# Expert walks: rounding the gated activations on ScalarE, with VectorE's remainder behind the first dot product

## The chip, the cores and the metric

The kernel runs on one core of a Trainium2 chip. The metric is device time in microseconds (us) of one execution. TensorE (PE) does the matrix products, VectorE (DVE) and ScalarE (ACT) the elementwise work, GpSimd (POOL) issues the indirect transfers and SyncE (SP) the plain ones. Each engine runs its own instructions in order and waits on semaphores for the others.

## What is computed

The reference is a two-layer backbone: in each layer a mixer (retention, convolution, long convolution) and then an expert layer over 16,384 single-neuron experts. The change touches the expert layer alone:

```python
q = (ht @ w_q).reshape(T, PEER_HEADS, 2, PEER_DKEY // 2)
...                                   # 16 experts for each of 8 heads: eb, with gates gb
def expert_block(args):
    hb, eb, gb = args
    a = jnp.einsum('tkd,td->tk', u_tab[eb], hb)
    w = (jax.nn.gelu(a.astype(jnp.float32)) * gb).astype(hb.dtype)
    return jnp.einsum('tk,tkd->td', w, v_tab[eb])
```

There are 512 latent tokens (and 256 context tokens in layer 0), each with 1024 features, all in 32-bit floats.

## The kernel before

The expert layer of each of the two layers is one stage, `stage_experts(l)`, which walks over NK = 128 blocks of 128 experts. 384 of the tokens are treated densely. For block k, `hidden(k)` multiplies the block of the u table with the activations (24 products of 128x384), ScalarE takes the gelu of the result into `w`, VectorE multiplies `w` by the dense gates `gt`, and `outputs(k)` multiplies it with the block of the v table and adds it up in six PSUM banks (18 products of 128x512). For accuracy every operand is split into two parts, a rounded one and its remainder: x_hi = round(x), x_lo = x - x_hi, and three products (hi hi, hi lo, lo hi) take the place of one. So a block needs `u_hi`/`u_lo`, `v_hi`/`v_lo` and `w_hi`/`w_lo`.

The remaining tokens are treated sparsely, in groups of 128: for each token the row of one chosen expert is gathered from memory (8 KB: its u and v parts), VectorE forms the dot product with the activation row (`dots`), ScalarE takes a small gelu and VectorE adds the weighted v part to the output row (`add_rows`). Layer 0 has two such groups (G = 2), layer 1 has one (G = 1). Four row buffers are in use, so a gather for step k+2 can be issued when `add_rows(k)` has read its buffer.

The order of the work is written out by hand for each engine, with waits on counted semaphores; there is no planner. In the steady part of the walk one step k is:

- VectorE, `step` (L2132): `weigh(k)` (gate product L2100, a drain, the rounding L2104 into `w_hi`, a drain, the remainder L2106 into `w_lo`, which raises `w_ready`), `dots(k)` (L2117, once for each group), `rest_u(k+2)` (L2085), `rest_v(k+1)` (L2090), `add_rows(k)` (L2125 and L2129, once for each group, which frees the row buffer).
- ScalarE, `step` (L2063): gelu of block k (L2067, waits for `hidden(k)`), `round_u(k+2)` (L2057, waits for the load of the u block), small gelu (L2071, waits for `dots(k)`), `round_v(k+1)` (L2061, waits for the load of the v block).
- TensorE, `step`: `hidden(k+1)`, then `outputs(k)`, which waits for `v_split` and `w_ready`.
- SyncE, `step` (L1984): load of the u block k+2 (L1987, 512 KB) once `hidden(k)` is done; load of the v block k+1 (L1991, 512 KB) once `outputs(k-1)` is done; and in every second step (k odd) a load of the gates for two blocks (L1981, 384 KB) once `w_ready` shows that `weigh(k)` is done. SyncE waits in this order, so the u load of the next step stands behind the wait of the gate load.
- GpSimd: G gathers (L2014), 1 MB each, each waiting for its row buffer.

Below, a *gate step* is a step k in which a gate load is issued (k odd), and a *plain step* is one in which none is. The u and v blocks have two buffers each.

The wait that ties the u load to the gate load is in these lines:

```python
if k % 2 == 1 and at_most(b, k, NK - 4):
    sp.wait_ge(w_ready.sem, w_ready.at(b + (k + 1)))
    load_gates(b, k + 3)
```

Of the kernel before, what the change touches and what calls it, by code (L numbers as in the profile page):

```python
# [7 lines left out]
F32 = mybir.dt.float32  # L8
U32 = mybir.dt.uint32
F32R = mybir.dt.float32r  # L10
ALU = mybir.AluOpType
# [45 lines left out]
def build(nc, xT, cT, ctxT, final_g, ada, mix, peer_u, peer_uv, peer_rows, peer_v, par, hw1, hw2, hw3, keys, k_mats, k_rope,  # L57
          k_dec, k_decc, k_feat_x, k_feat_c, k_win_x, k_win_c, k_dft_x, k_dft_c, out):
    stack = ExitStack()
    with stack:  # L60
# [13 lines left out]
        def new(name):  # L74
            return Count(nc, stack, name)
# [26 lines left out]
        rows_free, dots_ready, gelu_ready = new("expert_rows_free"), new("dots_ready"), new("small_gelu_ready")  # L102
        ctx_in, ctx_free, ctx_gelu = new("ctx_slots_loaded"), new("ctx_rows_free"), new("ctx_gelu_ready")
        ctx_rows_in = [new(f"ctx_rows_loaded_{k}") for k in range(6)]
        a_ready, a_free, o_done = new("hidden_ready"), new("hidden_read"), new("outputs_done")

        def flat(at, n):
# [1840 lines left out]
        def stage_experts(l):  # L1948
# [20 lines left out]
            def at_most(b, k, n):  # L1969

                return not isinstance(b, int) or b + k < n
# [5 lines left out]
            with nc.Block() as block:  # L1977
# [75 lines left out]
                @block.scalar  # L2053
                def _(act):
                    def round_u(b, k):
                        act.wait_ge(loaded[k % 2].sem, loaded[k % 2].at(8 * b + (16 * (k // 2) + 16)))
                        act.activation(u_ring_hi[:, k % 2, :], ring[:, k % 2, :], ACT.Copy).then_inc(u_hi.sem, 1)  # L2057

                    def round_v(b, k):
                        act.wait_ge(loaded[2 + k % 2].sem, loaded[2 + k % 2].at(8 * b + (16 * (k // 2) + 16)))  # L2060
                        act.activation(v_ring_hi[:, k % 2, :], ring[:, 2 + k % 2, :], ACT.Copy).then_inc(v_hi.sem, 1)  # L2061

                    def step(b, k):  # L2063
                        act.wait_ge(a_ready.sem, a_ready.at(b + (k + 1)))
                        if past(b, k, 2):
                            act.wait_ge(w_ready.sem, w_ready.at(b + (k - 1)))
                        act.activation(w[:, k % 2, :], ps[:, 6 + k % 2, 0:TD], ACT.Gelu_apprx_tanh).then_inc(a_free.sem, 1)  # L2067
                        if at_most(b, k, NK - 2):
                            round_u(b, k + 2)
                        act.wait_ge(dots_ready.sem, dots_ready.at(b + (k + 1)))  # L2070
                        act.activation(slot_g[:, G * k:G * k + G], slot_a[:, G * k:G * k + G], ACT.Gelu_apprx_tanh)\  # L2071
                           .then_inc(gelu_ready.sem, 1)
                        if at_most(b, k, NK - 1):
                            round_v(b, k + 1)

                    round_u(0, 0)
                    round_u(0, 1)
                    round_v(0, 0)
                    walk(act, step)

                @block.vector
                def _(dve):
                    def rest_u(b, k):
                        dve.wait_ge(u_hi.sem, u_hi.at(b + (k + 1)))
                        dve.tensor_tensor(ring_lo[:, k % 2, :], ring[:, k % 2, :], u_ring_hi[:, k % 2, :].bitcast(F32), ALU.subtract)\  # L2085
                           .then_inc(u_split.sem, 1)

                    def rest_v(b, k):
                        dve.wait_ge(v_hi.sem, v_hi.at(b + (k + 1)))
                        dve.tensor_tensor(ring_lo[:, 2 + k % 2, :], ring[:, 2 + k % 2, :], v_ring_hi[:, k % 2, :].bitcast(F32),  # L2090
                                          ALU.subtract).then_inc(v_split.sem, 1)

                    def weigh(b, k):

                        if k % 2 == 0:
                            half = (k // 2) % 2
                            dve.wait_ge(gates_in[half].sem, gates_in[half].at(4 * b + 16))
                        dve.wait_ge(a_free.sem, a_free.at(b + (k + 1)))
                        x, hi = w[:, k % 2, :], w_hi[:, k % 2, :]
                        dve.tensor_tensor(x, x, gt[:, (k // 2) % 2, k % 2, :], ALU.mult)  # L2100
                        dve.drain()
                        if past(b, k, 2):
                            dve.wait_ge(o_done.sem, o_done.at(b + (k - 1)))
                        dve.tensor_copy(hi, x)  # L2104
                        dve.drain()
                        dve.tensor_tensor(w_lo[:, k % 2, :], x, hi.bitcast(F32), ALU.subtract).then_inc(w_ready.sem, 1)  # L2106

                    def row_of(k, g):
                        return (G * k + g) % NBUF

                    def dots(b, k):

                        for g in range(G):
                            sem = rows_in[row_of(k, g)]
                            turn = 16 * ((G * k + g) // NBUF) + 16
                            dve.wait_ge(sem.sem, sem.at((16 * G // NBUF) * b + turn))
                            last = dve.tensor_tensor_reduce(rows[row_of(k, g)][:, 0:D], rows[row_of(k, g)][:, 0:D], h_rows[g], 1.0, 0.0, ALU.mult, ALU.add,  # L2117
                                                            slot_a[:, G * k + g:G * k + g + 1])
                        last.then_inc(dots_ready.sem, 1)

                    def add_rows(b, k):

                        dve.wait_ge(gelu_ready.sem, gelu_ready.at(b + (k + 1)))
                        here = slice(G * k, G * k + G)
                        dve.tensor_tensor(slot_w[:, here], slot_g[:, here], gates[:, ds(b + k, 1), :].rearrange("p a g -> p (a g)"),  # L2125
                                          ALU.mult)
                        dve.drain()
                        for g in range(G):
                            dve.scalar_tensor_tensor(o_rows[g], rows[row_of(k, g)][:, D:2 * D], slot_w[:, G * k + g:G * k + g + 1],  # L2129
                                                     o_rows[g], ALU.mult, ALU.add).then_inc(rows_free.sem, 1)  # L2130

                    def step(b, k):  # L2132
                        weigh(b, k)
                        dots(b, k)
                        if at_most(b, k, NK - 2):
                            rest_u(b, k + 2)
                        if at_most(b, k, NK - 1):
                            rest_v(b, k + 1)
                        add_rows(b, k)

                    rest_u(0, 0)
                    rest_u(0, 1)
                    rest_v(0, 0)
                    walk(dve, step)
            for k in range(4):
                loaded[k].add(16 * NK // 2)
            place[0] += 4
            for c in (a_ready, a_free, o_done, u_hi, v_hi, u_split, v_split, w_ready, dots_ready, gelu_ready):
                c.add(NK)
            for g in gates_in:  # L2150
                g.add(16 * NK // 4)
# [201 lines left out]
```

## Time and profile before

| | us |
|---|---|
| median of 3 runs | 6430.33 |
| the three runs | 6427.9, 6433.2, 6430.33 |
| the profiled execution, time | 6423.93 |
| the profiled execution, span from first to last instruction | 6422.1 |

| engine | busy us | share of the span | instructions |
|---|---|---|---|
| PE, products | 5309.5 | 83% | 24102 |
| PE, weight loads | 4083.9 | 64% | 24102 |
| DVE | 4402.1 | 69% | 7633 |
| ACT | 1714.8 | 27% | 2929 |
| POOL | 1100.2 | 17% | 824 |

The page also cuts the span into 40 equal slices of about 160 us and gives a digit for the busy tenths of each engine. The walk of layer 0 lies in slices 16 to 23, where the memory traffic stands at 370 to 372 GB/s; the walk of layer 1 lies in the last eight slices, at about 270 GB/s. Everything else (mixers, choice of experts, filters) is left as it is by the change.

### The profile page before, as it was taken

How to read it: one execution, taken by the hardware profiler on the slowest of the kernel's cores; microseconds unless marked ns; L12 is line 12 of the kernel's file. 1: busy time of each engine (PE TensorE's matmuls, PEld its weight loads, DVE VectorE, ACT ScalarE, POOL GpSimd, SP SyncE). 2: the span in 40 equal slices, each digit the busy share in tenths (PEclk: the TensorE clock that was granted, in tenths of full speed). 3: DMA queues.
4: the chain of work that ended last, by engine and by line, in shares of the span. 5: the costliest groups of instructions: out<-in, count | busy, mean ns of one | idle time of the engine just before them, and what ended most of it. 6: DMA issues, size and time to landing. Idle time of an engine off the chain costs nothing. (4 is left out here: it accounts for less than half of the span.)

```text
span 6422.1 us, 71090 instructions
## 1 busy us (share of the span) xinstructions
PE 5309.5 (83%) x24102; PEld 4083.9 (64%) x24102; DVE 4402.1 (69%) x7633; ACT 1714.8 (27%) x2929; POOL 1100.2 (17%) x824
## 2 busy tenths in 40 slices
PE   7787827887887777999999878977886559999998
PEld 5385726633355566888888737723475448999897
DVE  1347576758785787999999832358344987777776
ACT  1132211121022354222222211221022553333333
POOL 0003005505342001333333200005000001111110
PEclk8897868988998878999999979978998669999999
DMA  6141317701574356999999712201121247777775
GB/s 207 70 151 54 113 44 292 263 29 46 181 257 145 105 152 227 372 372 372 372 370 371 307 69 76 91 14 52 52 79 59 53 105 266 273 272 273 271 274 199
DMA packets 465497, 1180.24 MB, mean 184 GB/s; under 512 B 225436, under 2 KB 259645, under 8 KB 412543
## 3 DMA queue, kind: packets, MB, share of 16 engines
q1 hardware_dynamic: 373186, 641.52, 29.4%
q0 software_dynamic: 92160, 536.91, 22.3%
q8 instruction: 70, 1.15, 0.1%
q14 instruction: 81, 0.66, 0.0%
HBM read 1114.09 MB, written 64.23 MB: 183 GB/s over the span
## 5 line engine op out<-in xcount | busy, mean ns | idle before, releaser
L2014 POOL DMA_INDIRECT arena<-in_peer_uv,kept x384 | 522.2, 1360 | 3027.5 <-DVE arena L2129 1630.8
L220 PE MATMUL psum<-h_hi,ring_lo 128*128 128x384 f32 x2048 | 692.8, 338 | 0.0
L220 PE MATMUL psum<-h_lo,u_ring_hi 128*128 128x384 f32 x2048 | 692.3, 338 | 0.0
L220 PE MATMUL psum<-h_hi,u_ring_hi 128*128 128x384 f32 x2048 | 689.5, 337 | 0.0
L220 PE MATMUL psum<-v_ring_hi,w_hi 128*128 128x512 f32 x1536 | 618.5, 403 | 56.0 <-DVE w_lo L2106 56.0
L220 PE MATMUL psum<-ring_lo,w_hi 128*128 128x512 f32 x1536 | 605.2, 394 | 0.0
L220 PE MATMUL psum<-v_ring_hi,w_lo 128*128 128x512 f32 x1536 | 600.9, 391 | 0.0
L2057 ACT ACTIVATE u_ring_hi<-kept 128x1024 fp32r<-128x1024 f32 x256 | 271.7, 1062 | 1064.7 <-DMA kept<-in_peer_u 1052.7
L2129 DVE SCALAR_TENSOR_TENSOR arena<-arena 128x1024 f32<-128x1024 f32 x384 | 482.1, 1283 | 19.2
L2117 DVE CUSTOM_DVE_ANT_0 arena<-arena 128x1024 f32<-128x1024 f32 x384 | 458.8, 1220 | 0.1
L2090 DVE TENSOR_TENSOR ring_lo<-kept,v_ring_hi 128x1024 fp32r<-128x1024 f32 x256 | 313.7, 1226 | 202.6 <-ACT v_ring_hi L2061 191.9
L1629 PE MATMUL psum<-arena 128*128 128x128 f32 x1536 | 286.8, 346 | 147.8 <-DVE arena L1713 91.8
L220 PEld LDWEIGHTS psum<-h_hi,u_ring_hi 128*128 128x128 f32 x2048 | 384.6, 188 | 11.5 <-issue 0.5
L220 PEld LDWEIGHTS psum<-h_lo,u_ring_hi 128*128 128x128 f32 x2048 | 384.3, 188 | 10.8 <-issue 0.5
L220 PEld LDWEIGHTS psum<-v_ring_hi,w_hi 128*128 128x128 f32 x1536 | 289.0, 188 | 150.0 <-issue 94.4
L220 PEld LDWEIGHTS psum<-h_hi,ring_lo 128*128 128x128 f32 x2048 | 384.2, 188 | 0.0
L1110 PE MATMUL psum<-arena,kept 128*128 128x512 f32 (+1 forms) x768 | 305.8, 560 | 80.9 <-DVE arena L1156 63.9
L1629 PEld LDWEIGHTS psum<-arena 128*128 128x128 f32 x1536 | 248.8, 247 | 187.8 <-DVE arena L1713 128.7
L2085 DVE TENSOR_TENSOR ring_lo<-kept,u_ring_hi 128x1024 fp32r<-128x1024 f32 x256 | 312.9, 1223 | 47.9 <-ACT u_ring_hi L2057 47.1
L220 PEld LDWEIGHTS psum<-v_ring_hi,w_lo 128*128 128x128 f32 x1536 | 289.3, 188 | 70.2
L220 PEld LDWEIGHTS psum<-ring_lo,w_hi 128*128 128x128 f32 x1536 | 288.5, 188 | 53.5
L2061 ACT ACTIVATE v_ring_hi<-kept 128x1024 fp32r<-128x1024 f32 x256 | 269.7, 1053 | 180.4 <-DMA kept<-in_peer_uv 180.0
(343 smaller groups left out, 10444.2 us busy)
## 6 DMA issues: line engine op xcount, KB each, us to landing
kept<-in_mix SPq DMA_DIRECT2D x312, 512.0 KB
kept<-in_peer_u SPq DMA_DIRECT2D x256, 512.0 KB
kept<-in_peer_uv SPq DMA_DIRECT2D x256, 512.0 KB
kept<-in_ada SPq DMA_DIRECT2D x96, 512.0 KB
gate_scratch<-arena SPq DMA_DIRECT2D x12, 4096.0 KB, 20.8
arena<-gate_scratch SPq DMA_DIRECT2D x128, 384.0 KB
arena<-in_k_dft_x SPq DMA_DIRECT2D x6, 2048.0 KB
spec_scratch<-arena SPq DMA_DIRECT2D x4, 2048.0 KB, 8.5
```

Source lines behind the costliest of these rows:

```text
L220: done = pe.matmul(out, lhs[x], rhs[y], start=first and j == 0, stop=last and j == 2)
L1110: last = pe.matmul(ps[:, k, 0:T], ring[:, k, kc * P:(kc + 1) * P], x[:, kc, :], start=kc == 0, stop=kc == KC - 1)
L1629: last = pe.matmul(ps[:, n % 4, q * P:(q + 1) * P], hot_j[n % 3][:, q, :], hot_i[n % 3][:, q, :], start=True, stop=True)
L2014: pool.indirect_dma_start(rows[q % NBUF], None, peer_uv, bass.IndirectOffsetOnAxis(ap=row_id[q % G][:, q // G:q // G + 1], axis=0))\
L2057: act.activation(u_ring_hi[:, k % 2, :], ring[:, k % 2, :], ACT.Copy).then_inc(u_hi.sem, 1)
L2061: act.activation(v_ring_hi[:, k % 2, :], ring[:, 2 + k % 2, :], ACT.Copy).then_inc(v_hi.sem, 1)
L2085: dve.tensor_tensor(ring_lo[:, k % 2, :], ring[:, k % 2, :], u_ring_hi[:, k % 2, :].bitcast(F32), ALU.subtract)\
L2090: dve.tensor_tensor(ring_lo[:, 2 + k % 2, :], ring[:, 2 + k % 2, :], v_ring_hi[:, k % 2, :].bitcast(F32), ALU.subtract).then_inc(v_split.s ...
L2117: last = dve.tensor_tensor_reduce(rows[row_of(k, g)][:, 0:D], rows[row_of(k, g)][:, 0:D], h_rows[g], 1.0, 0.0, ALU.mult, ALU.add, slot_a[: ...
L2129: dve.scalar_tensor_tensor(o_rows[g], rows[row_of(k, g)][:, D:2 * D], slot_w[:, G * k + g:G * k + g + 1], o_rows[g], ALU.mult, ALU.add).th ...
```

## The change

ScalarE does the rounding into `w_hi` as a Copy activation of the same 128x384 tile, right after its gelu and ahead of `round_u(k+2)`; it waits for a new semaphore `weighed` that VectorE's gate product raises. VectorE's rounding and both drains of `weigh` are gone. The remainder `w_lo` becomes a function of its own, `rest_w`, which waits for a second new semaphore `w_rounded` and stands after the first dot product of the step: between the two dot products in layer 0 (G = 2), after the only one in layer 1 (G = 1). `w_ready` is raised by it as before. The wait for `outputs(k-2)`, which guards `w_hi`, moves with the rounding to ScalarE.

```diff
@@ ScalarE, step
                         act.activation(w[:, k % 2, :], ps[:, 6 + k % 2, 0:TD], ACT.Gelu_apprx_tanh).then_inc(a_free.sem, 1)
+                        act.wait_ge(weighed.sem, weighed.at(b + (k + 1)))
+                        if past(b, k, 2):
+                            act.wait_ge(o_done.sem, o_done.at(b + (k - 1)))
+                        act.activation(w_hi[:, k % 2, :], w[:, k % 2, :], ACT.Copy).then_inc(w_rounded.sem, 1)
                         if at_most(b, k, NK - 2):
                             round_u(b, k + 2)
@@ VectorE, weigh
                         dve.wait_ge(a_free.sem, a_free.at(b + (k + 1)))
-                        x, hi = w[:, k % 2, :], w_hi[:, k % 2, :]
-                        dve.tensor_tensor(x, x, gt[:, (k // 2) % 2, k % 2, :], ALU.mult)
-                        dve.drain()
-                        if past(b, k, 2):
-                            dve.wait_ge(o_done.sem, o_done.at(b + (k - 1)))
-                        dve.tensor_copy(hi, x)
-                        dve.drain()
-                        dve.tensor_tensor(w_lo[:, k % 2, :], x, hi.bitcast(F32), ALU.subtract).then_inc(w_ready.sem, 1)
+                        x = w[:, k % 2, :]
+                        dve.tensor_tensor(x, x, gt[:, (k // 2) % 2, k % 2, :], ALU.mult).then_inc(weighed.sem, 1)
+
+                    def rest_w(b, k):
+                        dve.wait_ge(w_rounded.sem, w_rounded.at(b + (k + 1)))
+                        dve.tensor_tensor(w_lo[:, k % 2, :], w[:, k % 2, :], w_hi[:, k % 2, :].bitcast(F32), ALU.subtract)\
+                           .then_inc(w_ready.sem, 1)
@@ VectorE, dots
                         for g in range(G):
+                            if g == 1:
+                                rest_w(b, k)
@@ VectorE, step
                         dots(b, k)
+                        if G == 1:
+                            rest_w(b, k)
```

## Rows read from the trace of the kernel before

**Rows 1.** Busy time by engine in a stretch of each walk: PE, PEld, DVE, ACT, POOL
```profile
2528.00:3653.00 1125.00, 1076.25 (x5249) 941.87 (x5248) 1083.94 (x1500) 323.33 (x499) 382.08 (x251) 1.00 0.96 371
5300.00:6300.00 1000.00, 993.97 (x4962) 897.46 (x4963) 744.61 (x1069) 316.15 (x474) 124.24 (x121) 1.00 0.78 272
```

**Rows 2.** Waits in 2700 to 3600 us: who for whom, total us, times, longest
```profile
PE psum L220 <- DVE w_lo L2106: 39.2, 100, 0.8
...
DVE ring_lo L2085 <- ACT u_ring_hi L2057: 0.6, 2, 0.5
```

**Rows 3.** Timeline of VectorE, gate step at 2689.76, plain step at 2698.75: start, duration
```profile
2689.76 0.55 DVE L2100 TENSOR_TENSOR arena<-arena 128x384 f32<-128x384 f32 x1
2690.38 0.45 DVE L2104 CAST w_hi<-arena 128x384 fp32r<-128x384 f32 x1
2690.91 0.56 DVE L2106 TENSOR_TENSOR w_lo<-arena,w_hi 128x384 fp32r<-128x384 f32 x1
2691.38 1.22 DVE L2117 CUSTOM_DVE_ANT_0 arena<-arena 128x1024 f32<-128x1024 f32 x1
...
2692.53 1.22 DVE L2117 CUSTOM_DVE_ANT_0 arena<-arena 128x1024 f32<-128x1024 f32 x1
...
2693.67 1.22 DVE L2085 TENSOR_TENSOR ring_lo<-kept,u_ring_hi 128x1024 fp32r<-128x1024 f32 x1
...
2698.75 0.55 DVE L2100 TENSOR_TENSOR arena<-arena 128x384 f32<-128x384 f32 x1
...
2702.66 1.22 DVE L2085 TENSOR_TENSOR ring_lo<-kept,u_ring_hi 128x1024 fp32r<-128x1024 f32 x1
...
2707.74 0.55 DVE L2100 TENSOR_TENSOR arena<-arena 128x384 f32<-128x384 f32 x1
```

**Rows 4.** Timeline of SyncE's queue in the same gate step
```profile
2691.64 0.38 SPq L1981 DMA_DIRECT2D arena<-gate_scratch  x1
2692.55 0.33 SPq L1987 DMA_DIRECT2D kept<-in_peer_u  x1
```

**Rows 5.** Timeline of ScalarE in the same two steps
```profile
2690.05 1.06 ACT L2057 ACTIVATE u_ring_hi<-kept 128x1024 fp32r<-128x1024 f32 x1 [3.72 <-DMA kept<-in_peer_u]
...
2701.30 1.06 ACT L2057 ACTIVATE u_ring_hi<-kept 128x1024 fp32r<-128x1024 f32 x1 [5.97 <-DMA kept<-in_peer_u]
```

**Rows 6.** Timeline: first and last of 61 gate steps, and the u load behind each
```profile
2545.77 0.55 DVE L2100 TENSOR_TENSOR arena<-arena 128x384 f32<-128x384 f32 x1
...
2557.65 1.06 ACT L2057 ACTIVATE u_ring_hi<-kept 128x1024 fp32r<-128x1024 f32 x1 [6.31 <-DMA kept<-in_peer_u]
...
3626.45 0.55 DVE L2100 TENSOR_TENSOR arena<-arena 128x384 f32<-128x384 f32 x1
...
3638.16 1.06 ACT L2057 ACTIVATE u_ring_hi<-kept 128x1024 fp32r<-128x1024 f32 x1 [6.16 <-DMA kept<-in_peer_u]
```

**Rows 7.** Line L1917: ScalarE's Copy of 128x384, ns min/median/max
```profile
L1917 ACT ACTIVATE h_hi<-arena x16: 506/509/526, 2480.5 to 5281.7; 128x384 fp32r<-128x384 f32 x16
```

**Rows 8.** Timeline of layer 1's SyncE queue: two u loads in a row
```profile
5806.53 0.33 SPq L1987 DMA_DIRECT2D kept<-in_peer_u  x1
...
5814.90 0.33 SPq L1987 DMA_DIRECT2D kept<-in_peer_u  x1
```

**Rows 9.** Memory traffic (last two columns) within the two steps of rows 3
```profile
2690.76:2692.76 2.00, 1.63 (x8) 1.17 (x7) 1.93 (x5) 0.36 (x1) 1.32 (x1) 1.00 0.80 215
2695.76:2707.76 12.00, 11.62 (x61) 10.52 (x60) 11.55 (x17) 2.59 (x4) 3.92 (x3) 1.00 1.01 405
```

**Rows 10.** GpSimd's second gather in the gate step of rows 3
```profile
2690.95 1.32 POOL L2014 DMA_INDIRECT arena<-in_peer_uv,kept  x1 [0.30 <-issue]
```

**Rows 11.** Gate step at 3013.93, its second gather, and the u load behind it
```profile
3013.93 0.55 DVE L2100 TENSOR_TENSOR arena<-arena 128x384 f32<-128x384 f32 x1
...
3015.81 1.78 POOL L2014 DMA_INDIRECT arena<-in_peer_uv,kept  x1 [0.98 <-issue]
...
3023.50 1.06 ACT L2057 ACTIVATE u_ring_hi<-kept 128x1024 fp32r<-128x1024 f32 x1 [4.00 <-DMA kept<-in_peer_u]
```

More of the change, by code:

```diff
@@ L104, in build @@
         ctx_rows_in = [new(f"ctx_rows_loaded_{k}") for k in range(6)]
+        weighed, w_rounded = new("hidden_weighed"), new("hidden_rounded")
         a_ready, a_free, o_done = new("hidden_ready"), new("hidden_read"), new("outputs_done")
@@ L2147, in stage_experts @@
             place[0] += 4
-            for c in (a_ready, a_free, o_done, u_hi, v_hi, u_split, v_split, w_ready, dots_ready, gelu_ready):
+            for c in (weighed, w_rounded, a_ready, a_free, o_done, u_hi, v_hi, u_split, v_split, w_ready, dots_ready, gelu_ready):
                 c.add(NK)
```

## The prediction

> **What bounds the kernel now.** The change lies in the two expert walks, so I read the busy time of each engine in a stretch of either walk first. In layer 1 TensorE is busy 994 of 1000 us and VectorE 745: TensorE is the bound [rows 1]. In layer 0 VectorE is busy 1084 of 1125 us, TensorE 1076, and the transfer engines stand at a share of 0.96: three resources within a few per cent of full [rows 1]. The waits show the order among them: TensorE waits for `w_lo` in every step (39.2 us in 100 steps, 0.39 each), VectorE for a rounded u block only twice [rows 2]. Before the change, layer 0 therefore runs at the speed of VectorE's own list.
>
> The timeline of VectorE gives that list: from the gate product of one step to that of the next it is 8.99 us, almost without a gap [rows 3]. Over 120 steps the mean is (3626.45 - 2545.77) / 120 = 9.005 [rows 6], so 18.01 us for a gate step and a plain step together. This pair is the unit below, since SyncE's list repeats every two steps.
>
> The last view is the one that decides: when does each u block land, against when it is wanted? The u block whose load is issued in the plain step is rounded from 2690.05 to 2691.11 and its remainder starts at 2693.67, 2.6 us to spare [rows 3, 5]. The u block whose load stands behind the gate load is another matter: issued at 2692.55 [rows 4], landed at 2701.30, rounded by 2702.36, wanted by VectorE at 2702.66 [rows 3, 5]: 0.30 us to spare. Measured from the gate product of its gate step it lands 11.54 us later; in the first and the last of 61 such pairs the distance is 11.88 and 11.71 [rows 6], and the mean over the 61 is 11.56.
>
> **The change, part by part.**
>
> *VectorE's list.* Before, gate product to `rest_u` is 3.91 us: 0.62 to the rounding, 0.53 to the remainder, 0.47 to the first dot product, 1.15 and 1.14 for the two [rows 3]. After, the gate product hands over after 0.47 (the start-to-start of the equal tensor-tensor L2106), then 1.15, the remainder 0.47, and 1.14: 3.23. So 0.68 us fewer, and the list needs 8.99 - 0.68 = 8.31. The two new waits hold it up only if ScalarE is late: the Copy of this shape takes 0.51 [rows 7]; from 0.55 it is done at about 1.15, the remainder is due at 1.62. ScalarE is busy 323 of 1125 us [rows 1] and waits at that moment for a u block or for `dots`; 0.51 more costs nothing.
>
> *TensorE.* Its floor is layer 1's period, 5814.90 - 5806.53 = 8.37 [rows 8]. `w_ready` comes 2.18 us after the gate product (0.47 + 1.15 + 0.56) instead of 1.71: 0.47 later. In the steady state that alone is harmless, since the gate product itself may come earlier.
>
> *SyncE, the queue that the change is moved past.* The gate load waits for `w_ready`, and the next u load stands behind it. Both are issued 0.47 later after the gate product: the gate load at 2.35 instead of 1.88 [rows 3, 4].
>
> *The u block behind the gate load, new bound.* After it lands, 1.06 us of rounding and about 0.04 of hand-over pass, and from that `rest_u` to the gate product of the next gate step it is 2707.74 - 2702.66 = 5.08 [rows 3]. With L as the distance from gate product to landing, a pair cannot be shorter than L + 1.10 + 5.08. With the old L of 11.56 that is 17.74 us. VectorE's 16.62 and TensorE's 16.74 are out of reach: most of the 1.36 us that VectorE saves in a pair becomes waiting for this block. The question is only whether L keeps still. Call its shift x; a pair is then 17.74 + x, against 18.01 before, and the point of no change is x = 0.27.
>
> *What moves L.* First, the later gate load. Around it the traffic is only 215 GB/s, while from 6 to 18 us of the pair it is 405 at a full share [rows 9]. 0.47 us at the lower rate instead of the full one delays (405 - 215) / 405 x 0.47 = 0.22 us of transfer; the ends are 0 (the gathers use the gap fully) and 0.47. Second, the plain step now begins 8.31 instead of 8.99 us after the gate product, and its two gathers of 1 MB each with it, 0.68 us earlier, while the u block is still in flight. If the gathers took the whole traffic in that time, the block would land 0.68 later; if its bytes were already through, 0. I take two thirds, 0.45: a gather's row is 8 KB against 4 KB for a row of the block. That this order matters, one row shows: in the gate step at 3013.93 the second gather started 1.88 instead of 1.19 us after the gate product, and the u block landed 9.57 instead of 11.56 us after it [rows 10, 11]. A gather 0.7 us later gave 2.0 us; the mirror image, the gathers relatively earlier by as much, is the far end of x, 0.22 + 2.0 = 2.2.
>
> So x = 0.22 + 0.45 = 0.67, a pair 18.41. There are 62 pairs with a gate load (k odd up to 123): 62 x 0.40 = +25 us.
>
> A page of the Trainium skill, "DMA: Bandwidth & Descriptors", section "Where 436 GB/s comes from", holds that transfers from HBM are bound at about 358 GB/s for a core, which speaks against any gain here; by that rule a step with its 3.34 MB would take 9.3 us, before and after. The trace does not agree: it holds 371 over 1125 us and 405 over 12 us [rows 1, 9]. The measurement decides, and the bound is taken from 405.
>
> *Ends of the walks.* In the last step of each walk TensorE has nothing left but `outputs`, and the 0.47 lies open: +1 us for both. *Layer 1.* TensorE is full there and its period stays; VectorE's idle 25% hides the later `w_ready`. 0.
>
> **Sum.** +25 + 1 = +26 us. The profiled execution took 6423.93 (span 6422.1), 6.4 below the median; its own time would become 6450, and the median 6430.33 + 26 = 6456.
>
> **The rivals.**
>
> 1. *The full gain.* The u block follows the faster step, as if its landing were tied to VectorE's list, and layer 0 becomes bound by TensorE like layer 1: 125 steps x (9.005 - 8.37) = 79 us, less 1: 6352. For it: traffic of 3.34 MB in 8.37 us is 399 GB/s, under 405. Against it: 0.30 us to spare [rows 3 to 5] where 0.68 a step would be needed twice, less what the load gives. Chance 0.08.
> 2. *The landing keeps still* (x near 0, under 0.06): a pair of 17.74, 62 x 0.27 = 17 us less, plus 1: 6414. For it: a landing set by bytes, not by the moment of issue. Chance 0.17.
> 3. *A balance* (x from 0.06 to 0.46): within 13 us of before. The removed VectorE time is found again as VectorE's wait for the u block. A traffic that is already full gives the same, 6431: the trace's 371 GB/s over the walk may be all that this mix of transfers reaches, against the 405 over 12 us [rows 1, 9]; I give that 0.05 of this rival's chance of 0.25. The bandwidth rule of the Trainium skill's "DMA: Bandwidth & Descriptors" would come out as this case.
> 4. *The forecast, the other side of 1 and 2:* one mechanism, the u load queued behind the gate load, with its price x above 0.46. Chance 0.50, of which 0.08 for more than +65 us (x over 1.3).
>
> That ScalarE's rounding be late enough to hold VectorE at `rest_w` is excluded by 0.5 us of room a step.
>
> **How the numbers follow.** The likeliest is the forecast, 6456; its own range is 6443 to 6495. With the balance and the small gain, and with the far end of x cut where 0.08 is left, the range is 6405 to 6495; the full gain is left out. About 0.2%, 13 us, is what a measurement of this kernel can tell from no change: faster 0.25, same 0.25, slower 0.50.
>
> **What the changed profile would show.** Right: VectorE's L2085 waits for L2057 in about every second step, about 1.8 us each, in all over 100 us in the layer-0 walk; the list from gate product to `rest_u` takes 3.23 in gate steps; gate and plain steps differ (8.3 and 10.1); TensorE waits for `w_lo` still; layer 1 keeps 8.37. Wrong: L2085 without waits and a period near 8.4 (rival 1); L at or under 11.56 (rival 2); waits at `rest_w` for the rounding; or waits for v blocks in layer 0, which showed none and which I have not priced.

## The result and the profile after

The change makes the kernel slower by over 3%, some eight times the loss that was forecast.

| | before | after |
|---|---|---|
| median, us | 6428.87 (6 runs, 6419.52 to 6433.2) | 6631.62 (6 runs, 6606.17 to 6644.68) |
| ratio, with its 95% interval | | 1.0318 (1.0302 to 1.0334) |
| span of the profiled execution, us | 6422.1 | 6624.1 |
| mean granted clock of TensorE | 0.895 | 0.889 |

Busy time by engine in a stretch of each walk, after (columns PE, PEld, DVE, ACT, POOL, granted clock, transfer share, GB/s), to be held against [rows 1]:

```profile
2528.00:3653.00 1125.00, 985.67 (x4620) 869.55 (x4619) 901.69 (x1211) 337.61 (x550) 333.27 (x221) 0.94 0.88 326
5500.00:6400.00 900.00, 852.64 (x4214) 759.34 (x4215) 584.53 (x807) 302.15 (x504) 101.07 (x100) 1.00 0.73 256
```

In layer 0 no resource is full any more: TensorE fell from 1076 to 986 us, VectorE from 1084 to 902, the traffic from 371 to 326 GB/s. Layer 1 had TensorE at 99%; it is at 95% now. When everything has room and the time is longer, the kernel runs at the speed of a loop of latencies. The granted clock, full before, is 0.94 in layer 0.

The step periods say how much is lost where. A *pair* is a gate step and the plain step behind it; all periods here are means over 62 gate and 62 plain steps, read from the gate products in the timeline.

| us | gate step | plain step | pair | against before, x 62 |
|---|---|---|---|---|
| layer 0 before | 8.99 | 9.02 | 18.01 | |
| layer 0 after | 8.31 | 12.00 | 20.31 | +142 |
| layer 1 before | 7.93 | 8.83 | 16.76 | |
| layer 1 after | 6.44 | 11.35 | 17.79 | +64 |

Together +206, where the spans differ by 202. The waits in the layer-0 walk (2700 to 3600 us; who for whom, total us, times, longest) name what is late, where before there were 0.39 us a step for `w_lo` and nearly nothing else [rows 2]:

```profile
PE psum L221 <- DVE w_lo L2109: 111.7, 43, 4.1
ACT v_ring_hi L2062 <- DMA kept<-in_peer_uv: 108.0, 37, 5.6
DVE ring_lo L2095 <- ACT v_ring_hi L2062: 105.3, 37, 5.5
DVE ring_lo L2090 <- ACT u_ring_hi L2058: 61.9, 44, 1.6
```

and in layer 1 (5400 to 6300 us):

```profile
DVE ring_lo L2095 <- ACT v_ring_hi L2062: 167.6, 46, 4.1
DVE ring_lo L2090 <- ACT u_ring_hi L2058: 124.2, 49, 3.6
...
PE psum L221 <- DVE w_lo L2109: 44.0, 44, 1.7
```

Once a pair, VectorE waits for the u block, then for the v block, and then TensorE for `w_lo`. The wait for the v block is the larger one in both walks.

One pair of layer 0 in the timeline (start, duration; SPq and POOL rows are issues of transfers), the gate step at 3141.66 and the plain step at 3149.95, against [rows 3 to 5]. At 22.53 us it is one of the longer pairs; the mean is 20.31. Where a load is said to land, it is the start of ScalarE's rounding, which waits for it; where ScalarE did not wait, that is only the latest time at which it can have landed.

```profile
3141.66 0.55 DVE L2105 TENSOR_TENSOR arena<-arena 128x384 f32<-128x384 f32 x1
...
3142.25 0.52 ACT L2072 ACTIVATE w_hi<-arena 128x384 fp32r<-128x384 f32 x1 [4.01 <-DVE arena L2105]
...
3143.28 0.55 DVE L2109 TENSOR_TENSOR w_lo<-arena,w_hi 128x384 fp32r<-128x384 f32 x1
...
3143.97 0.47 PE L221 MATMUL psum<-v_ring_hi,w_hi 128*128 128x512 f32 x1 [2.13 <-DVE w_lo L2109]
...
3145.48 0.63 PE L221 MATMUL psum<-ring_lo,w_hi 128*128 128x512 f32 x1
3145.90 0.63 PE L221 MATMUL psum<-v_ring_hi,w_lo 128*128 128x512 f32 x1
...
3149.33 0.39 PE L221 MATMUL psum<-ring_lo,w_hi 128*128 128x512 f32 x1
3149.56 0.39 PE L221 MATMUL psum<-v_ring_hi,w_lo 128*128 128x512 f32 x1
3149.79 0.34 PE L221 MATMUL psum<-h_hi,u_ring_hi 128*128 128x384 f32 x1
...
3150.14 0.33 SPq L1992 DMA_DIRECT2D kept<-in_peer_uv  x1
...
3159.33 1.06 ACT L2062 ACTIVATE v_ring_hi<-kept 128x1024 fp32r<-128x1024 f32 x1 [4.87 <-DMA kept<-in_peer_uv]
...
3160.42 1.23 DVE L2095 TENSOR_TENSOR ring_lo<-kept,v_ring_hi 128x1024 fp32r<-128x1024 f32 x1 [4.79 <-ACT v_ring_hi L2062]
...
3164.19 0.55 DVE L2105 TENSOR_TENSOR arena<-arena 128x384 f32<-128x384 f32 x1
```

Read it as a ring. `w_ready` comes 2.17 us after the gate product (3143.83). 0.14 later the outputs start and take 5.82. The v load goes out 0.35 after them, lands after 9.19, is rounded and waited for in 1.09, and 3.77 later stands the gate product of the next gate step. 2.17 + 0.14 + 5.82 + 0.35 + 9.19 + 1.09 + 3.77 = 22.53, the whole of 3164.19 - 3141.66. Such a sum of distances closes by itself. What makes the ring the bound is that each link starts only when the one before it ends: the rows show TensorE idle for `w_lo` (2.13 us), ScalarE for the v block (4.87) and VectorE for ScalarE (4.79), and VectorE runs from `rest_v` to the next gate product almost without a gap. It goes once round in two steps, because the v block that is loaded is the one for two blocks later.

The outputs need 5.82 us instead of 18 x 0.234 = 4.21 because the clock is low at their head: their products start 0.43 apart until 3147.6 and 0.23 apart after. By stretches of the same pair:

```profile
3141.66:3144.66 3.00, 0.87 (x5) 0.58 (x4) 3.00 (x6) 1.47 (x2) 2.20 (x2) 0.95 0.52 176
3144.66:3149.95 5.29, 5.29 (x18) 4.21 (x17) 5.14 (x7) 1.53 (x3) 0.84 (x1) 0.70 0.97 327
3149.95:3164.19 14.24, 12.59 (x66) 11.49 (x65) 8.23 (x12) 3.12 (x5) 3.04 (x3) 1.00 0.85 318
```

The granted 0.70 in the middle is a mixture of the two levels, 1.2 and 2.4 GHz, behind an idle TensorE. This is not so in every pair: in 27 of the 62 the outputs took 5.6 to 7.0 us, all behind a wait of TensorE of 2.1 us or more, and in the other 35 they took 4.24.

With the full clock the ring is 11.73 us + the time of the v landing in layer 0. In layer 1 the list behind the v block is shorter (2.57 for 3.77) and `w_ready` comes at 2.16, so it is 10.53 + landing. Here is where layer 1's time goes (a gate step at 6003.47):

```profile
6003.82 1.01 POOL L2015 DMA_INDIRECT arena<-in_peer_uv,kept  x1 [11.01 <-DVE arena L2135]
...
6009.62 1.01 POOL L2015 DMA_INDIRECT arena<-in_peer_uv,kept  x1 [4.79 <-DVE arena L2135]
...
6010.36 0.33 SPq L1992 DMA_DIRECT2D kept<-in_peer_uv  x1
...
6018.16 1.06 ACT L2062 ACTIVATE v_ring_hi<-kept 128x1024 fp32r<-128x1024 f32 x1 [3.96 <-DMA kept<-in_peer_uv]
```

and the same in the kernel before:

```profile
5810.89 1.01 POOL L2014 DMA_INDIRECT arena<-in_peer_uv,kept  x1 [7.96 <-DVE arena L2129]
...
5818.64 1.01 POOL L2014 DMA_INDIRECT arena<-in_peer_uv,kept  x1 [6.73 <-DVE arena L2129]
...
5819.06 0.33 SPq L1991 DMA_DIRECT2D kept<-in_peer_uv  x1
...
5823.70 1.06 ACT L2061 ACTIVATE v_ring_hi<-kept 128x1024 fp32r<-128x1024 f32 x1 [1.52 <-DMA kept<-in_peer_uv]
```

The gathers follow each other after 7.75 us before and after 5.80 us now, and the v block takes 7.80 instead of 4.64. Over the walk: of 60 v blocks that ScalarE waited for after the change all took more than 6 us, and 59 of them had a gather 0.7 us ahead of the load and, 5.8 us ahead of that, the gather before it. Before, 98 of 111 took less than 5 us, at a mean spacing of about 8.2; the 13 that took 5 to 8 had a spacing of 7.3. The gather just ahead of the load isn't enough by itself: before the change 15 v blocks had one less than 1 us ahead, but with the gather before that over 8 us earlier, and took 4.1 to 4.6 us. Means for plain steps: 4.73 before, 7.35 after. The ring then gives 10.53 + 7.35 = 17.88, and the pair of layer 1 measures 17.79. Before, with `w_ready` 0.51 earlier, 10.53 - 0.51 + 4.73 = 14.75 lay under TensorE's 16.74.

In layer 0 the links of the ring, as means over the 62 pairs, are 2.16 + 0.15 + 5.08 + 0.35 + 7.71 + 1.09 + 3.77 = 20.31. Against the same distances before, 0.45 of the 2.30 us a pair is the later `w_ready`, 0.84 the slower outputs (5.08 for 4.24) and 0.99 the v block (7.71 for at most 6.72, which nothing waited for). VectorE waits for the v block in 51 of the 62 pairs.

### The profile page after: what moved, and what is told of

Read it like the earlier page. It is cut to its first block and busy times, and to the rows that moved or that the text cites. A ratio compares the mean times of both kernels' runs of the same rounds, so it can differ in the third digit from the quotient of the medians.

```text
span 6624.1 us, 70740 instructions
## 1 busy us (share of the span) xinstructions
PE 5363.4 (81%) x24102; PEld 4125.7 (62%) x24102; DVE 4279.9 (65%) x7377; ACT 1820.0 (27%) x3185; POOL 1086.8 (16%) x824
## 5 line engine op out<-in xcount | busy, mean ns | idle before, releaser
L221 PE MATMUL psum<-v_ring_hi,w_hi 128*128 128x512 f32 x1536 | 641.8, 418 | 210.5 <-DVE w_lo L2109 210.3
L221 PE MATMUL psum<-ring_lo,w_hi 128*128 128x512 f32 x1536 | 625.4, 407 | 0.0
L221 PE MATMUL psum<-v_ring_hi,w_lo 128*128 128x512 f32 x1536 | 620.2, 404 | 0.0
L221 PEld LDWEIGHTS psum<-v_ring_hi,w_hi 128*128 128x128 f32 x1536 | 302.8, 197 | 308.2 <-issue 248.1
L2072 ACT ACTIVATE w_hi<-arena 128x384 fp32r<-128x384 f32 x256 | 134.6, 526 | 874.5 <-DVE arena L2105 874.5
```

The lines of the kernel that those rows point to most:

```text
L221: done = pe.matmul(out, lhs[x], rhs[y], start=first and j == 0, stop=last and j == 2)
L2072: act.activation(w_hi[:, k % 2, :], w[:, k % 2, :], ACT.Copy).then_inc(w_rounded.sem, 1)
```

## The experiments

The gate step, the plain step and the ring above left four suspects: the remainder's place, the gate load's place, the gathers' place, and the clock. All results, with the means of a pair in the profiled execution (that of e1 took 6471 us and was the fastest of its four, 42 us under their median; that of e10 lies 29 us under its median, the others within 19 us of theirs). The kernel before was measured again beside each group of experiments (medians 6419.5 to 6422.5 us), so what an edit gives back is read from the ratios:

| kernel | ratio to before (95%) | pair, layer 0 | pair, layer 1 |
|---|---|---|---|
| after | 1.0318 (1.0302 to 1.0334) | 20.31 | 17.79 |
| e2_rest_at_once | 1.0002 (0.9989 to 1.0014) | 18.12 | 16.78 |
| e3_rest_behind_alone | 1.0295 (1.0264 to 1.0326) | 19.87 | 17.86 |
| e1_gates_on_weighed | 1.0162 (1.0128 to 1.0197) | 18.50 | 17.27 |
| e7_gate_load_late | 1.0007 (0.9997 to 1.0017) | 18.05 | 16.77 |
| e5_gather_after_outputs | 1.0069 (1.0040 to 1.0097) | 19.22 | 16.72 |
| e9_both_orders | 1.0049 (1.0033 to 1.0066) | 18.68 | 16.73 |
| e6_clock_filler | 1.0235 (1.0213 to 1.0258) | 19.81 | 17.49 |
| e4_filler | 1.1296 (1.1270 to 1.1322) | 30.44 | 17.54 |
| e8_mixed | 0.9995 (0.9983 to 1.0008) | 18.22 | 16.81 |
| e10_mixed_ordered | 1.0012 (0.9998 to 1.0026) | 17.98 | 16.72 |
| e12_no_gate_loads | 0.9976 (0.9963 to 0.9990) | 17.83 | 16.71 |
| e13_before_no_gate_loads | 1.0002 (0.9990 to 1.0013) | 18.04 | 16.75 |

### Which half of the change: e2 and e3

e2: ScalarE rounds, as in the change, but the remainder follows at once.

```diff
@@ VectorE, dots (against after)
                         for g in range(G):
-                            if g == 1:
-                                rest_w(b, k)
@@ VectorE, step
                         weigh(b, k)
+                        rest_w(b, k)
                         dots(b, k)
-                        if G == 1:
-                            rest_w(b, k)
```

> Only the first half of the change: ScalarE rounds, VectorE takes the remainder at once, ahead of the first dot product. w_ready then comes at 0.55 + 0.05 + 0.52 + 0.05 + 0.55 = 1.7 us after the gate product, as before the change, and VectorE's list is about as long as before (it waits 0.65 for ScalarE). Theories G and V both: the loss goes, 6430 within 0.5%. Rival S (the u rounding queued on ScalarE behind the new rounding, or the hand-overs between the engines, cost the time): it stays slow, above 6550.

Measured 6422.26 us: no change. VectorE then waits for the rounding, 0.59 a step, and gives back what its list saved:

```profile
DVE w_lo L2109 <- ACT w_hi L2072: 59.2, 100, 0.6
```

e3: VectorE keeps the rounding, only the remainder goes behind the first dot product.

```diff
@@ VectorE, weigh (against before; dots and step as in the change)
-                        dve.tensor_copy(hi, x)
-                        dve.drain()
-                        dve.tensor_tensor(w_lo[:, k % 2, :], x, hi.bitcast(F32), ALU.subtract).then_inc(w_ready.sem, 1)
+                        dve.tensor_copy(hi, x).then_inc(w_rounded.sem, 1)
+
+                    def rest_w(b, k):
+                        dve.wait_ge(w_rounded.sem, w_rounded.at(b + (k + 1)))
+                        dve.tensor_tensor(w_lo[:, k % 2, :], w[:, k % 2, :], w_hi[:, k % 2, :].bitcast(F32), ALU.subtract)\
+                           .then_inc(w_ready.sem, 1)
```

> Only the second half, on the kernel before: VectorE still rounds, but the remainder stands behind the first dot product. w_ready comes at 0.62 + 0.4 + 1.15 + 0.56 = 2.7 us after the gate product, 0.55 later than in the changed kernel; VectorE's list is 0.15 to 0.5 shorter than before. Theories G and V: as slow as the changed kernel or slower, 6600 to 6800. Rival S: near 6430.

Measured 6604.15 us: nearly the whole loss, in both layers, without ScalarE in it. So ScalarE's part is innocent, and the remainder's later place is the cause. What it delays is `w_ready`, which in e3 comes 2.68 us after the gate product in layer 0 and 2.64 in layer 1. The ring of layer 1 gives 11.00 + 6.81 (its plain v landing) = 17.81, measured 17.86. The loss is not in proportion to the delay: `w_ready` is 0.97 us later than before in layer 0 here and 0.45 in the changed kernel, at nearly the same loss, since the v block takes 6.96 us here and 7.71 there.

### The gate load: e1 and e7

e1: in the changed kernel the gate load, and with it the u load behind it, waits for the gate product instead of `w_ready`.

```diff
-                            sp.wait_ge(w_ready.sem, w_ready.at(b + (k + 1)))
+                            sp.wait_ge(weighed.sem, weighed.at(b + (k + 1)))
```

> The changed kernel, with the gate load waiting for the gate product (weighed) instead of for w_ready; the gate table is read by nothing else. Theory G (the gate load behind the late w_ready, with the next u load queued behind it, makes the blocks late): the gate load goes out at about 0.7 us after the gate product instead of 2.35 and the pair of steps falls from 20.3 to below 18 us in layer 0 and from 17.8 to 16.8 in layer 1, time 6350 to 6430. Rival V (the later w_ready delays outputs, and with it the v load that waits for outputs; the gate load only adds bytes): the v load is not helped, VectorE still waits for v in plain steps, time above 6550.

Measured 6512.78 us, ratio 1.0162 for 1.0318: about half of the loss comes back, and the time lies between the two expectations. At first sight this is what the forecast's mechanism asks for: in layer 0 VectorE's wait for the u block falls from 1.37 to 0.34 us a plain step. But layer 1, in which the forecast saw no loss, gains half of its share too, and the plain v landing there is 6.66 instead of 7.35 (10.53 + 6.66 = 17.19, measured 17.27). The test of the forecast's mechanism is therefore the other one. e7: the kernel before, with the gate load held back to the end of the dot products, much further than the change holds it.

```diff
-                            sp.wait_ge(w_ready.sem, w_ready.at(b + (k + 1)))
+                            sp.wait_ge(dots_ready.sem, dots_ready.at(b + (k + 1)))
```

> The kernel before, with one edit: the gate load waits for the dot products of its step instead of for w_ready, so it and the u load behind it go out about 2.2 us later in layer 0 (4.1 instead of 1.9 us after the gate product) and 1.2 later in layer 1. w_ready and VectorE's list are as before. Theory G (the gate load's queue place alone is enough to make blocks late): VectorE waits for u blocks in plain steps of layer 0 by 1.5 to 2 us, time 6530 or more. Rival V (w_ready and the outputs behind it are what count): below 6470.

Measured 6425.08 us: nothing. A gate step of layer 0 in it:

```profile
2680.38 0.55 DVE L2100 TENSOR_TENSOR arena<-arena 128x384 f32<-128x384 f32 x1
...
2684.54 0.38 SPq L1981 DMA_DIRECT2D arena<-gate_scratch  x1
2685.46 0.33 SPq L1987 DMA_DIRECT2D kept<-in_peer_u  x1
...
2691.90 1.06 ACT L2057 ACTIVATE u_ring_hi<-kept 128x1024 fp32r<-128x1024 f32 x1 [5.96 <-DMA kept<-in_peer_u]
```

The u load goes out 5.08 us after the gate product and lands 11.52 after it. Over 61 pairs the issue stands at 4.91 us where before it stood at 2.62, and the landing at 11.53 where before it was at 11.56. The landing doesn't follow the issue at all. That the other transfers in flight set it is argued; it fits that in e13 below, where no gate load stands ahead of it, the block lands 8.06 us after the gate product (issued at 1.66). In the kernel before, the forecast's term for the later gate load is zero. e1's gain appears only in the changed kernel, where the v block is waited for: its mean time in layer 0's plain steps goes from 7.71 to 6.48 us. Which part of that gain comes over the u block and which over the v block no run separates.

### The gathers: e5, e9

e5: the changed kernel, with the gather that refills the buffers of block j also waiting for `outputs(j)`, so that it can't run ahead of the v load.

```diff
                             pool.wait_ge(rows_free.sem, rows_free.at(q - NBUF + 1))
+                            pool.wait_ge(o_done.sem, o_done.at((q - NBUF) // G + 1))
```

> The changed kernel, in which each gather also waits until TensorE has finished outputs of the step whose row buffer it takes, the same event for which SyncE issues the v load; so a gather no longer goes out ahead of the v load of the plain step (0.75 us ahead in layer 1). Theory O (order in the queues: the 8 KB gather rows ahead of the v block stretch its 4.5 us to 7.8): the v wait of the plain steps in layer 1 falls from 3.2 us to under 1.5 and layer 1's pair from 17.8 towards 17, time 6560 to 6600; layer 0, where the gather is issued a microsecond ahead too, gains as well. Rival (the gather's moment does not matter, only the bytes): 6620 or more.

Measured 6468.99 us, ratio 1.0069 for 1.0318: nearly four fifths of the loss, about 160 us, come back by holding a transfer *back*, more than was expected. Layer 1 is whole again, TensorE busy for every microsecond of the stretch:

```profile
5500.00:6300.00 800.00, 800.00 (x4012) 725.13 (x4011) 562.07 (x765) 295.06 (x477) 114.52 (x95) 1.00 0.79 274
```

```profile
5806.48 1.16 POOL L2016 DMA_INDIRECT arena<-in_peer_uv,kept  x1 [7.38 <-PE psum L221]
...
5814.26 0.33 SPq L1992 DMA_DIRECT2D kept<-in_peer_uv  x1
...
5814.85 1.06 POOL L2016 DMA_INDIRECT arena<-in_peer_uv,kept  x1 [7.22 <-PE psum L221]
...
5818.81 1.06 ACT L2063 ACTIVATE v_ring_hi<-kept 128x1024 fp32r<-128x1024 f32 x1
```

The gathers are 8.37 us apart and behind the v load, which is down within 4.55 us (mean of plain steps 4.52). The u block may come late now (VectorE waits 1.7 us for it a plain step); TensorE hides it. Layer 0 keeps 1.21 us a pair of its loss, at a v block of 6.85 us in the mean of its plain steps and outputs of 4.62.

e9 has both edits, e1's and e5's.

> The changed kernel with both edits to the order of the transfers: the gate load waits for the gate product, and each gather waits for outputs of its step as the v load does. Theory O+G (the order of the transfers is what the change upset; each of the two edits repairs a part, one alone left 6469 and 6513): layer 1 at 8.36 a step, layer 0's pair from 19.2 to 17.6 to 18.2, time 6400 to 6440. Rival (layer 0 is short of transfer capacity, whatever the order): the pair stays above 18.7, time above 6455.

Measured 6451.04 us, 1.0049, with a pair of 18.68 us: short of the 6400 to 6440 of the theory and close to the rival. The interval overlaps with that of e5, so beside the gathers' order the gate load's place adds little that is shown. The gains of e1 and e5 do not add up; both act on the same ring. With both orders repaired the change still loses 0.3 to 0.7%.

### The clock: e4 and e6

e4: sixteen products of zeros ahead of the outputs of each gate step of layer 0, so that TensorE isn't idle while it waits.

```diff
+                        if G == 2 and k % 2 == 1:
+                            for n in range(16):
+                                pe.matmul(ps[:, n % 6, :], zeros[:, 0:P], zeros, start=False, stop=False)
```

> The changed kernel with 16 products of zeros (128x512, added to the sums, 3.7 us at full clock) on TensorE ahead of outputs in the gate steps of layer 0 alone, where TensorE waits 2 to 4 us for w_ready and then runs its first products at half clock (0.63 us instead of 0.39). Theory C (the wait lets the clock fall, outputs take 6 instead of 4.2 us, the v load that waits for them goes out 2 us late, and this keeps the wait alive): the pair in layer 0 falls from 20.3 to under 19 us, time 6520 to 6560, layer 1 as it was. Rival (the clock is only a symptom): time 6620 or more.

Measured 7248.92 us. It decided nothing: the filler was mis-sized. A product of plain float32 leaves two records of 592 ns, 0.43 apart, so sixteen took 13.9 us, where TensorE's wait was 2.4 us in the mean and 4.1 at most:

```profile
L2036 PE MATMUL psum<-arena 128*128 128x512 f32 x2048 | 889.3, 592 | 0.0
```

The full clock that it held is all that it tells. e6 does it with operands in the form of the others: fifteen products of 128x384 (2.6 us) at the head of `hidden`, overwritten by it.

```diff
+                        if G == 2 and k % 2 == 0 and past(b, k, 2):
+                            for kc in range(5):
+                                c = slice(kc * P, (kc + 1) * P)
+                                pe_products(pe, ps[:, 6 + k % 2, 0:TD], (u_ring_hi[:, k % 2, c], ring_lo[:, k % 2, c]),
+                                            (h_hi[:, kc, :], h_lo[:, kc, :]), kc == 0, kc == 4)
```

> The changed kernel, in which TensorE runs 15 extra products (128x384 at 0.175 us, 2.6 us; their sum is overwritten) at the head of hidden in the gate steps of layer 0, into the gap in which it waits for w_ready. The filler of the run before took 13.9 us and decided nothing. Theory C (the wait lets TensorE's clock fall, outputs take 6 us for 4.2, the v load behind them is late, and this keeps the wait alive): products of outputs in gate steps back at 0.39 us, the pair of layer 0 falls from 20.3 to under 19, time 6520 to 6570. Rival (the clock is a symptom, the filler costs its own time): pair 20 or more, 6620 or more.

Measured 6568.95 us: added work makes the kernel faster, by 53 us by the ratios (1.0235 for 1.0318). The clock is full and the wait for `w_lo` (2700 to 3600) 14 us instead of 112:

```profile
2560.00:3500.00 940.00, 923.36 (x4693) 843.15 (x4692) 775.56 (x1041) 292.64 (x474) 285.80 (x190) 1.00 0.90 338
```

```profile
PE psum L221 <- DVE w_lo L2114: 14.1, 14, 1.9
```

By the pairs, 62 x 0.50 = 31 us of that are layer 0's; another 19 fell in layer 1, whose code is the same in both, and the changed kernel's own runs differ by 38 us. So only the 31 us of layer 0 can be put down to the filler, and its pair of 19.81 us is over the 19 that the theory asked for and under the 20 of its rival. The links of the ring say why: the outputs go from 5.08 to 4.19 us, back at the full rate, but they start 0.79 us later behind the filler, and the v block takes 7.31 instead of 7.71. The low clock thus costs 0.84 us a pair in the changed kernel (52 us over the walk), and filling the gap gives back 0.50 after its own price.

### What VectorE's shorter list is worth: e8, e10, e12, e13

e8 puts the remainder behind the first dot product only in layer 0's plain steps, whose `w_ready` no gate load waits for, with e1's edit; e10 adds e5's.

```diff
                         for g in range(G):
-                            if g == 1:
+                            if g == 1 and k % 2 == 0:
                                 rest_w(b, k)
@@ VectorE, step
                         weigh(b, k)
-                        dots(b, k)
-                        if G == 1:
+                        if G == 1 or k % 2 == 1:
                             rest_w(b, k)
+                        dots(b, k)
```

> A version meant to be faster than both: the changed kernel with the gate load waiting for the gate product, the remainder at once in all steps of layer 1 and in the gate steps of layer 0, and behind the first dot product only in the plain steps of layer 0. VectorE's list is then 8.99 + 8.31 = 17.3 us a pair, w_ready in gate steps as early as before. Theories G and V together: pair 17.3 to 17.7 in layer 0, layer 1 as before, time 6385 to 6415. If the transfers are simply full: 6430 or more.

> The mixed version (gate load behind the gate product; remainder at once in layer 1 and in the gate steps of layer 0, behind the first dot product in the plain steps of layer 0) with the gathers waiting for outputs as well. The mixed version alone stood at 6420 with a pair of 18.2 in layer 0 and 0.35 us of waiting for u and for v in plain steps. Theory O+G: the waits go, pair 17.4 to 17.9, time 6385 to 6410. If layer 0 is short of transfer capacity: 6415 to 6430.

Measured 6420.25 and 6430.19 us, both level with before; the gains that were hoped for (6385 to 6415) did not come, and no version of the change that does the whole work beat the kernel before. In e10 VectorE's busy time is lower than before (865 against 906 of the same 940 us), the ring is broken (v waits of 0.16 a plain step), and the pair is 17.98 against 18.01 even in this fast execution. What stands near full is the transfers, at a share of 0.98:

```profile
2560.00:3500.00 940.00, 896.54 (x4413) 794.23 (x4412) 865.37 (x1160) 325.16 (x527) 318.62 (x210) 1.00 0.98 374
```

To see whether bytes are the limit, e12 takes the gate loads of layer 0 out of the kernel of e5 (the first four blocks' gates serve for all later ones; 393 KB fewer a pair), and e13 out of the kernel before. VectorE's wait for the gates and its count, not shown, are changed to match.

```diff
-                        if k % 2 == 1 and at_most(b, k, NK - 4):
+                        if G == 1 and k % 2 == 1 and at_most(b, k, NK - 4):
                             sp.wait_ge(w_ready.sem, w_ready.at(b + (k + 1)))
                             load_gates(b, k + 3)
```

> The changed kernel with its gathers held behind the outputs of the right block, as before, and with no gate loads in layer 0's walk beyond those of the first four blocks: the later blocks use the gates of the first four, which is 393 KB fewer a pair of steps (some 6.7 MB become 6.3 MB). Theory 'the transfers of layer 0 are full': at the 374 GB/s that the mixed and ordered kernel moved, a pair takes 6.29/374 = 16.8 us where the kernel before takes 18.0, and the list of VectorE (8.3 + 8.3 = 16.6 of a pair) lies under it, so 62 pairs give some 62 x 1.2 = 74 us: about 6350 to 6370 us, a ratio near 0.99. Rival 'the two-step loop over latencies, not bytes': the outputs, the landing of the v block, rest_v and the weights still come late, the bytes taken away change nothing of it, and the time stays at 6440 us or above (that of the ordered kernel, 6469, less the share of the gate load's place). Layer 1 is left as it is in the ordered kernel, at 8.36 us a step.

> The kernel before, with no gate loads in layer 0's walk beyond those of the first four blocks: the later blocks use the gates of the first four. Theory 'the transfers of layer 0 are full only where VectorE's list is shorter': the kernel before is at its list of 8.99 us a step there, so fewer bytes bring nothing: 6410 to 6430 us, a ratio within 0.2% of 1. Rival 'the gate loads hold the kernel before back too': it gets faster by over 0.3%, below 6408 us.

e13 measured 6420.44 us, as expected: before the change, VectorE's list is the bound and the gate loads cost nothing. e12 measured 6400.8 us, between the two expectations. About 60 us under e5 by the ratios (0.9976 for 1.0069) come with the gate loads' absence, so they did feed the ring; but the 6350 to 6370 of a limit in bytes isn't reached. The two rows of e12 (the stretch, and its waits for gathered rows):

```profile
2560.00:3500.00 940.00, 896.57 (x4411) 794.28 (x4410) 864.06 (x1156) 325.98 (x526) 319.99 (x210) 1.00 0.96 352
```

```profile
DVE arena L2124 <- DMA arena<-in_peer_uv,kept: 54.2, 64, 1.9
```

The share of transfer time is still 0.96 while the rate is down to 352 GB/s, and VectorE now waits for the gathers, 0.54 a step, in place of u and v. The transfer queues of e12 and of before show who fills that share (2700 to 3600 us; packets, MB, share), e12 first:

```profile
q0 software_dynamic: 28940, 210.76, 65.3%
...
q1 hardware_dynamic: 29010, 105.60, 30.1%
```

```profile
q0 software_dynamic: 28789, 209.71, 60.6%
q1 hardware_dynamic: 42289, 124.16, 35.4%
```

The same bytes of gathers take 65.3% instead of 60.6% of the engines' time. So a full share stands at 352 GB/s here and at 371 before: no single figure in GB/s is the limit. Why the gathers take longer, no run here tells, and that the transfers bound layer 0 in e10 and e12 is argued from the share.

## Why the prediction was wrong, point by point

The sign was forecast, the size was not: 6456 with a range to 6495, measured 6631.62. The likeliest case named the wrong load, so that its sign came out right is in good part luck. The step that failed is the one that called the later `w_ready` harmless and left the v blocks unpriced; the runs showed a ring over the v load in its place, in both layers.

- *VectorE's list 8.99 to 8.31, 3.23 to `rest_u`.* Right: the gate step takes 8.31 in the mean, and in the timeline `rest_u` starts 3.23 us after the gate product in gate steps.
- *ScalarE's rounding at no cost.* Right: 0.52 us from 0.59 on, and VectorE never waits for it at `rest_w`; e2 and e3 confirm that it has no part in the loss.
- *`w_ready` 0.47 later, "in the steady state that alone is harmless".* This is the first step that failed. It is a link of the ring `w_ready`, outputs, v load, landing, remainder, gate product. Only the path over the gate load was followed from it.
- *The v blocks, "not priced".* The largest term was missing, and it could have been set up from the trace at hand: outputs 4.2, issue 0.35, rounding 1.1, list 3.8, `w_ready` 2.2. That gives 11.7 + landing in layer 0, hence room for a landing of 6.7 us in the forecast pair of 18.41, where before it took up to 6.7. The forecast itself stood at the edge of a second bound. After the change the v block took 7.71 in the mean. The forecast did name waits for v blocks as a sign of being wrong, and that sign came.
- *"Layer 1: 0".* Failed by 64 us. "VectorE's idle 25% hides the later `w_ready`" takes a share for a slack. The ring had 16.74 - 14.75 = 2.0 us of room there, and 13 of 111 v landings before were already 5 to 8 us long. Before, such a landing passed; with 0.51 less room it delays a step, the next gathers come 5.8 us after the last, and the following v block is late again. e5 and e9, which move the gathers behind the v load and further apart, show that their timing keeps this going; that single late landings start it is argued from the sum, not shown.
- *The u block behind the gate load, x = 0.67.* The mean landing went from 11.56 to 11.98 after the gate product (x = 0.42). But the term for the gate load (0.22) is zero in e7, and the wait for u (1.37 a plain step, forecast 1.8) is followed by a longer one for v, so it isn't what sets the pair. The row at 3013.93 [rows 11] was one row: in the changed kernel the gather of the same step is as late (1.88), and the u block lands 0.55 us ahead of the mean there, not 2.0. The thought behind it, that a gather's place has a price, was right, and the gathers' place was the largest lever. It was applied to one load only, though v loads and gathers are released by neighbouring events.
- *The clock.* Not thought of. [Rows 1] have it full, and the forecast gave TensorE an idle time in every pair without asking what follows. It cost 0.84 us a pair in the outputs, 52 us.
- *Rival 3's full traffic.* It was given 0.05 and is the nearest to what bounds layer 0 once the ring is broken: e10 stands at 374 GB/s and a share of 0.98, level with before. The figure of about 358 GB/s a core in the Trainium skill's "DMA: Bandwidth & Descriptors", section "Where 436 GB/s comes from", isn't a bound here (371 and 374 over 900 us and more). e12 shows a share of 0.96 at 352.

## What to carry to other kernels

For each signal that a change makes later, walk every ring that it is part of: from the signal over the loads that its consumer releases, back to the signal, in as many steps as there are buffers, and hold the sum against the period. An engine's idle share says nothing about the slack of such a ring; here 25% idle stood beside 2.0 us. If faster release of buffers sends big transfers out in bunches, tie them to the same event as the small load that others wait for: holding the gathers back won about 160 us.

## What the runs showed of the hardware

- A 512 KB block load takes about 4.5 us where the 1 MB gathers are 8.4 us apart and behind it, and 7 to 8 us where one stands 0.75 ahead of it and 5.8 behind the last, at a transfer share that is 0.73 on the whole.
- With one gather less than 1 us ahead of the load but the gather before it over 8 us earlier, the block load took 4.1 to 4.6 us (15 loads of the kernel before, layer 1).
- Issuing a gate load and the u load behind it 2.29 us later moved the u block's landing by -0.03 us, in a stretch with a transfer share of 0.97.
- In 27 of 62 pairs, each behind a wait of TensorE of 2.1 to 4.1 us, products of 128x512 started 0.43 us apart instead of 0.23 at the head of the outputs, in the pair shown in a stretch whose granted clock was 0.70; in the other 35, behind waits of 0.35 to 3.5 us, the clock stayed full.
- A 128x512 product of plain float32 operands took 0.87 us, against 0.23 for one of rounded operands.
